# Modulation as row sums of a feature-major table, the first norm by feature blocks, five units fed as the chunks come

## The reference

```python
mod = c @ ada_w[l] + ada_b[l]                      # 1024 -> 6 * 1024
sh1, sc1, gt1, sh2, sc2, gt2 = [m[:, None, :] for m in jnp.split(mod, 6, axis=-1)]
h = rmsnorm(x, norm1_g[l]) * (1.0 + sc1) + sh1
p = h @ w_in[l]
xr, yr, q, k, v, ga, gb = jnp.split(p, cuts, axis=-1)
q = head_rmsnorm(q.reshape(b_, s_, ATT_HEADS, HEAD_DIM), q_norm_g[l])
k = head_rmsnorm(k.reshape(b_, s_, ATT_HEADS, HEAD_DIM), k_norm_g[l])
y_b = stick_breaking_attention(q, k, v)            # strictly causal, suffix sums of log(1 - beta)
mix = jax.nn.sigmoid(ga) * y_a + jax.nn.sigmoid(gb) * y_b
x = x + gt1 * (mix @ w_out[l])
h2 = rmsnorm(x, norm2_g[l]) * (1.0 + sc2) + sh2    # the second norm, then the feed-forward part
```

## Time and profile before

| | us |
|---|---|
| runs | 1677.64, 1678.43, 1678.77; median 1678.43 |
| the profiled execution | 1679.01, of which span 1677.2 |
| granted TensorE clock, mean over the span | 0.988 of full speed |
| busy: PE, DVE, ACT, POOL | 1631.8, 1001.8, 805.3, 811.4 |
| read from HBM | 163.45 MB, 99 GB/s over the span |
| first product of a unit | 42.63 |

### The profile page before, as it was taken

One profiled execution on the slowest core, in us unless ns is written; L12 is line 12 of the kernel. 1 busy time (PEld: TensorE's weight loads), 2 busy tenths in 40 slices (PEclk: granted clock), 3 DMA queues, 4 the chain that ended last, 5 costly groups with the idle time before them and its releaser, 6 DMA issues.

```text
span 1677.2 us, 19574 instructions
## 1 busy us (share of the span) xinstructions
PE 1631.8 (97%) x7252; PEld 1331.1 (79%) x7252; DVE 1001.8 (60%) x1172; ACT 805.3 (48%) x1010; POOL 811.4 (48%) x583
## 2 busy tenths in 40 slices
PE   3999999999999999999999999999999999999997
PEld 2778787777778888888888888888888888888885
DVE  6687898878657728616634767566337554255541
ACT  2565666666544324424352333677554444244442
POOL 2254454454645545455565454554584352453525
PEclk7999999999999999999999999999999999999999
DMA  9333332443323233233233231211132221321312
GB/s 372 126 123 127 124 116 77 138 138 100 101 82 103 90 109 100 88 125 100 90 100 95 76 107 62 73 56 57 64 99 77 63 88 55 109 88 52 100 50 76
DMA packets 46462, 166.81 MB, mean 99 GB/s; under 512 B 5152, under 2 KB 5280, under 8 KB 45856
## 3 DMA queue, kind: packets, MB, share of 16 engines
q1 hardware_dynamic: 46368, 165.57, 29.8%
HBM read 163.45 MB, written 2.10 MB: 99 GB/s over the span
## 4 chain that ended last, share of the span: by engine, by line
PE 91%; DVE 5%; ACT 1%; DMA 1%; issue 1%; POOL 1%; SPq 0%; POOLq 0%; ACTq 0%; DVEq 0%
PE lin L658 17%; PE lin L660 16%; PE lin L659 16%; PE big L659 7%; PE big L658 7%; PE big L660 7%; DVE scr L1611 1%; PE big L771 1%; PE m_o L789 1%; PE big L1076 1%; PE big L1078 1%; PE big L1077 1%; DMA scr<-ada 1%; DVE scr L1719 1%; PE m_a L964 1%
## 5 line engine op out<-in xcount | busy, mean ns | idle before, releaser
L624 POOL TENSOR_TENSOR w_lo<-raw,w_hi 128x512 fp32r<-128x512 f32 x200 | 291.5, 1458 | 622.0 <-ACT w_hi L1115 621.7
L658 PE MATMUL lin<-h_hi,w_hi 128*128 128x512 f32 x936 | 370.4, 396 | 2.1 <-POOL w_lo L627 1.9
L660 PE MATMUL lin<-h_hi,w_lo 128*128 128x512 f32 x936 | 365.4, 390 | 0.0
L659 PE MATMUL lin<-h_lo,w_hi 128*128 128x512 f32 x936 | 365.2, 390 | 0.0
L627 POOL TENSOR_TENSOR w_lo<-raw,w_hi 128x512 fp32r<-128x512 f32 x209 | 309.9, 1483 | 13.9 <-ACT w_hi L1115 13.9
L1115 ACT ACTIVATE w_hi<-raw 128x1024 fp32r<-128x1024 f32 (+1 forms) x209 | 217.6, 1041 | 203.0 <-DMA raw<-weights 52.1
L658 PEld LDWEIGHTS lin<-h_hi,w_hi 128*128 128x128 f32 x936 | 176.2, 188 | 41.1 <-issue 2.7
L659 PEld LDWEIGHTS lin<-h_lo,w_hi 128*128 128x128 f32 x936 | 176.1, 188 | 38.1 <-issue 2.2
L660 PEld LDWEIGHTS lin<-h_hi,w_lo 128*128 128x128 f32 x936 | 176.0, 188 | 37.2
L624 POOL TENSOR_TENSOR qk_hl<-raw,qk_hl 128x512 fp32r<-128x512 f32 x43 | 59.9, 1392 | 126.8 <-ACT qk_hl L1115 126.8
L658 PE MATMUL lin<-y_hi,w_hi 128*128 128x512 f32 x260 | 101.5, 391 | 0.0
(11 more groups left out here) (507 smaller groups left out, 3401.1 us busy)
## 6 DMA issues: line engine op xcount, KB each, us to landing
raw<-weights SPq DMA_DIRECT2D x245, 512.0 KB, 3.5
slab<-ada SPq DMA_DIRECT2D x32, 512.0 KB, 4.4
scr<-ada SPq DMA_DIRECT2D x16, 512.0 KB, 6.3
raw<-weights SPq DMA_DIRECT2D x10, 256.0 KB, 2.7
x<-x_t SPq DMA_DIRECT2D x2, 1024.0 KB, 6.4
out_t<-scr SPq DMA_DIRECT2D x8, 256.0 KB, 2.6
raw<-weights SPq DMA_DIRECT2D x4, 448.0 KB, 3.4
rgw<-rg_w SPq DMA_DIRECT2D x1, 1024.0 KB, 8.6
```

The source lines that it names most:

```text
L624: nc.gpsimd.tensor_tensor(lo[:, 0:4 * P], raw[:, s, 0:4 * P], hi[:, 0:4 * P].bitcast(F32), ALU.subtract).then_inc(w_half, 1)
L658: nc.tensor.matmul(psum_of(n), wh, hi(k), start=(k == 0), stop=False)
L659: nc.tensor.matmul(psum_of(n), wh, lo(k), start=False, stop=False)
L660: last = nc.tensor.matmul(psum_of(n), wl, hi(k), start=False, stop=(k == nk - 1))
```

## The change

Five things change together.

1. *The table is turned.* The host lays `ada_w` out feature-major: a chunk now holds 128 output features on the partitions and all 1024 values of c's index on the columns. One DVE instruction, `tensor_tensor_reduce`, multiplies it by c, written out along every row, and adds up the row, with the bias as the start (`modulate`). The accumulators, PE's one-column products and the additions of the bias go. c's row is made at the start: DVE spreads c over the diagonal (`c_spread`), two products with ones turn it (`c_turned`), ACT copies it to SBUF (`c_copied`). The first 16 sums read it from PSUM, the later 32 from SBUF.
2. *The first norm by blocks.* The chunks come as scale 0, shift 0, scale 1, shift 1 and so on. DVE makes two sums and then the h block, eight times. The root is written to PSUM, and the blocks read it there.
3. *Five units at once.* PE takes q0, k0, v0, q1 and k1 chunk by chunk as the blocks come, by a table (`LANES`). v0, q1 and k1 get the three banks of `big`, and two more homes for weights lie in y_hi and y_lo. The first five packs are loaded between the modulation chunks.
4. *Order in head 1.* v1 comes before the scores of head 0, which wait for the copies of q1 and k1 as well; ACT copies k1 before it takes up the scores. Chunks 16 to 18 stand behind v1 in the ring, 19 to 21 between xr0 and yr0.
5. *Fillers.* Three products after the squares and twelve behind the second norm's sum (`keep_clock`), whose results nobody reads. Small: the constants are loaded in two parts, x signals in two halves, DVE's small preparations stand before the sums.

The diff, cut to its core:

```diff
@@ ring_plan @@
-            units += [("q", 0, 8), ("k", 0, 8), ("v", 0, 8), ("ada", a, 8), ("ada", a + 1, 8), ("q", 1, 8),
-                      ("ada", a + 2, 8), ("k", 1, 8), ("ada", a + 3, 8), ("v", 1, 8), ("ada", a + 4, 8)]
+            units += [("q", 0, 8), ("k", 0, 8), ("v", 0, 8), ("q", 1, 8), ("k", 1, 8), ("v", 1, 8)]
+            units += [("ada", a + i, 8) for i in range(3)] + [("xr", 0, 8)] + [("ada", a + i, 8) for i in (3, 4)]
             continue
...
+TABLE = [b for k in range(DK) for b in (DK + k, k)] + list(range(ADA_FIRST, NADA))
+SIDE = {("v", 0): 2, ("q", 1): 3, ("k", 1): 4}
+
+LANES = ((("q", 0), (1, 2, 3, 4, 5, 6, 7, 8)), (("k", 0), (0, 2, 3, 4, 5, 6, 7, 8)),
+         (("v", 0), (0, 0, 3, 4, 5, 6, 7, 8)), (("q", 1), (0, 0, 0, 0, 3, 6, 7, 8)),
+         (("k", 1), (0, 0, 0, 0, 0, 0, 3, 8)))
@@ SP @@
             for i in range(ADA_FIRST):
+                if i in (0, 2, 4, 9, 12):
+                    load_weights((0, 2, 4, 9, 12).index(i))
@@ PE @@
+            def keep_clock(n, bank, ones, moving):
+
+                for _ in range(n):
+                    nc.tensor.matmul(bank, ones, moving, start=True, stop=True)
...
-            modulation(0)
-            modulation(1)
+            keep_clock(3, lin[:, 0], c_("ones"), x[:, 0])
+            for step in range(DK):
+                pe.wait_ge(h_low, step + 1)
+                for (kind, j), due in LANES:
+                    for k in range(due[step - 1] if step else 0, due[step]):
+                        chunk(kind, j, k)
...
-                if h == 0:
-                    pair(("q", 0), ("k", 0), H, L, normed(0))
-                elif h < HEADS:
+                if h > 1:
                     unit("q", h, H, L)
-                if h == 1:
-                    unit("k", h, H, L)
+                if g == 0:
+                    unit("v", h, H, L)
                 if g >= 0:
                     pe.wait_ge(kq_normed, 2 * g + 2)
                     if g > 0:
                         pe.wait_ge(gates_read, g)
+                    else:
+                        pe.wait_ge(q_copied, 2)
+                        pe.wait_ge(k_copied, 2)
                     scores(g)
...
-                    if h % 2 == 0:
-                        modulation(1 + h // 2)
...
             norm_sum(0)
-            modulation(5)
+            keep_clock(12, m_o[:], ones_r[:], y_hi[:, 0])
@@ ACT @@
+                if k == 3:
+                    act.wait_ge(c_turned, 1)
+                    nc.scalar.activation(c_row, c_row_ps, ACT.Copy).then_inc(c_copied, 1)
+                    act.wait_ge(c_copied, 1)
+            norm_root(square_used, 8, D, m_a[:])
+            for k in range(DK):
+                if k in (0, 1, 2):
+                    split_ahead(0, k)
+                if k in (4, 5):
+                    split_ahead(0, k - 1)
+                high(0, k)
...
+                if h < 2:
+                    keys(h)
                 if g >= 0:
                     act.wait_ge(z_done, g + 1)
@@ DVE @@
-            def accumulate(a):
+            def modulate(i):
...
+                v.tensor_tensor_reduce(out=src, in0=src, in1=row, scale=scale, scalar=first, op0=M, op1=AD,
+                                       accum_out=to).then_inc(ada_used, 1)
+                dve.wait_ge(ada_used, counted(ada_used))
...
+            dve.wait_ge(c_copied, 1)
+            for k in range(DK + 1):
+                if k < DK:
+                    modulate(2 * k)
+                    modulate(2 * k + 1)
+                    if k == 0:
+                        dve.wait_ge(norm_rooted, 1)
+                    v.scalar_tensor_tensor(out=tmp[:, k % 4], in0=x[:, k], scalar=sm(A1 + k), in1=m_a[:],
+                                           op0=M, op1=M).then_inc(pre_h, 1)
+                    dve.wait_ge(pre_h, counted(pre_h))
+                if k > 0:
+                    e = k - 1
+                    dve.wait_ge(h_high, e + 1)
+                    v.scalar_tensor_tensor(out=h_lo[:, e], in0=tmp[:, e % 4], scalar=sm(MOD + e),
+                                           in1=h_hi[:, e].bitcast(F32), op0=AD, op1=SU).then_inc(h_low, 1)
+                    dve.wait_ge(h_low, counted(h_low))
...
                 else:
-                    accumulate(ADA_FIRST)
-                    accumulate(ADA_FIRST + 1)
+                    modulate(ADA_FIRST)
...
-                accumulate(ADA_FIRST + 4 * h + 2)
+                modulate(ADA_FIRST + 4 * h + 1)
+                modulate(ADA_FIRST + 4 * h + 2)
```

More of the change, by code:

```diff
@@ L180, in bank_plan @@
         if kind in ("rv", "vn"):
+            continue
+        if (kind, j) in SIDE:
+            bank[n], before[n] = SIDE[kind, j], None
+            last[bank[n]] = n
             continue
@@ L211, in build @@
         par_loaded = sem("par_loaded")
-        x_loaded = sem("x_loaded")
+        x_loaded = [sem(f"x_loaded{i}") for i in range(2)]
         cst_loaded = sem("cst_loaded")
+        diff_loaded = sem("diff_loaded")
         rgw_loaded = sem("rgw_loaded")
@@ L716, in norm_sum @@
                     .then_inc(norm_summed, 1)
-            def modulation(g):
-                pe.wait_ge(acc_ready, g + 1)
-                acc = acc_first if g == 1 else acc_even
-                for m in range(DK):
-                    out = m_o[:, 8 * g + m:8 * g + m + 1] if g < 2 else m_b[:, 8 * g - 16 + m:8 * g - 15 + m]
-                    last = nc.tensor.matmul(out, acc[:, m // 4, (m % 4) * P:(m % 4 + 1) * P], c_("ones")[:, 0:1],
-                                            start=True, stop=True)
-                last.then_inc(mod_done, 1)
             def pair(a, b, hi, lo, ready):
@@ L757, in normed, with chunk @@
                 return ready
+            def chunk(kind, j, k):
+                n = UNIT[(kind, j)]
+                if k == 0:
+                    pe.wait_ge(w_split, PACK[n] + 1)
+                w_h, w_l = weights_of(n)
+                wh, wl = w_h[:, k * P:(k + 1) * P], w_l[:, k * P:(k + 1) * P]
+                nc.tensor.matmul(psum_of(n), wh, H(k), start=(k == 0), stop=False)
+                nc.tensor.matmul(psum_of(n), wh, L(k), start=False, stop=False)
+                last = nc.tensor.matmul(psum_of(n), wl, H(k), start=False, stop=(k == DK - 1))
+                if k == DK - 1:
+                    last.then_inc(unit_done, 1)
             pe.wait_ge(cst_loaded, 16)
-            pe.wait_ge(par_loaded, 16)
+            pe.wait_ge(c_spread, 1)
+            for i in range(2):
+                last = nc.tensor.matmul(m_bo[:, i], c_("ones"), c_row[:, i * T:(i + 1) * T], start=True, stop=True)
+            last.then_inc(c_turned, 1)
             for k in range(DK):
                 square(k + 1, k == 0, k == DK - 1)
-            modulation(0)
-            modulation(1)
+            keep_clock(3, lin[:, 0], c_("ones"), x[:, 0])
[4 more added lines that the diff above has]
+                        chunk(kind, j, k)
             def scores(g):
@@ L1190, in gate, with high @@
                 act.wait_ge(rgate_done, counted(rgate_done))
-            def highs(r):
-                for k in range(DK):
-                    act.wait_ge(pre_h, DK * r + k + 1)
-                    nc.scalar.activation(h_hi[:, k], tmp[:, k % 4], ACT.Identity,
-                                         bias=sm(MOD + 24 * r + k)).then_inc(h_high, 1)
-                    act.wait_ge(h_high, counted(h_high))
+            def high(r, k):
+                act.wait_ge(pre_h, DK * r + k + 1)
+                nc.scalar.activation(h_hi[:, k], tmp[:, k % 4], ACT.Identity,
+                                     bias=sm(MOD + 24 * r + k)).then_inc(h_high, 1)
+                act.wait_ge(h_high, counted(h_high))
             act.wait_ge(consts_set, 2)
@@ L1328, in _ @@
             norm_root(norm_summed, 1, D)
-            highs(1)
+            for k in range(DK):
+                high(1, k)
             for t in range(THIRDS):
```

140 lines of the change are left out of this document (65 added, 75 removed).

## The result

The changed kernel takes 1685.17 us (median of 5 runs, 1681.40 to 1686.51) against 1678.43 before: 6.7 us more, ratio 1.0036, 95% interval 1.0025 to 1.0047. 1678.0 was forecast. The profiled execution is the slowest of the five: 1686.51, span 1684.5, 7.3 more than the span before.

The account below looks back on a forecast made before the run. TensorE, busy 97% of 1677.2 us, was taken as the bound. Front +5.0, modulation products -5.1 and fillers -0.3 gave -0.4 us, so 1678.0; the forecast's own range was 1674.5 to 1681.5, the wider one 1666 to 1684.

Parts of the forecast that it names:

- the front: Everything up to head 0's turned weights: 2.8 us behind, plus 2.2 for the low clock, summed to +5.0 us.
- Part 1: Modulation and first norm on DVE: steps of 4.5 us, five units complete at 61.7 instead of 74.47, a 12.8 us lead.
- Part 2: Behind the five units: head 0's scores wait for q1 and k1, start 4.7 us late; turned weights 2.8 us behind.
- the pack named: yr 0's weight pack, loaded behind chunks 19 to 21, holds ACT before q1's copy some 8 us; 4.70 from issue to start.
- The 2.2 us for the clock: Behind the wait at head 0's turned weights, PE stays at the low clock level, costing 2.2 us more.
- Part 3: After the front: three groups of modulation products gone from the full PE stage, -5.1 us; fillers -0.3; the rest nothing.
- Twelve fillers: Products of 0.23 us in the wait for the second norm, keeping 2.4 GHz at best: 0.3 us won.
- (1): Rival at head 0's scores: yr's pack is there in time, the lead stays, scores start at 69.0; 1665 us, chance 0.15.
- (2): Rival on the front's sums: they are short, 1.23 us, with 17 on the path, 4.1 us less; 1674 us, chance 0.17.
- (3): Rival: accumulating sums halve in speed; 1681 us if only three behind q0, 1696 if all 17; chance 0.13.
- (4): Rival: PE at 1.2 GHz into the fifth step, or both waits cost 6 us of low level; 1682, shared chance 0.10.

Follow-up runs that it names:

- experiments 1 and 2: Ring of two PSUM banks started at bank 1 instead of 0: in the changed kernel, 1681.50 us; in the kernel before, 1681.55 us.
- Kernel 9: Changed kernel with ring started at bank 1, yr0's pack ahead of chunks 19 to 21, first half of x in two transfers, head 1 reordered: 1667.86 us.
- kernel 4: Changed kernel with both repairs: ring of two banks started at bank 1, yr0's weight pack loaded ahead of chunks 19 to 21; 1671.35 us.
- experiment 8: Against kernel 4: ACT splits yr0's pack behind q1's and k1's copies, DVE builds the low part of k1's squares ahead of the shares; 1668.73 us.
- experiments 5 and 6: Two runs against kernel 4: first half of x in two smaller transfers, 1669.98 us; both groups of filler products taken out, 1672.06 us.
- experiment 7: Against kernel 4: the sixteen modulation sums of the front read c's row from SBUF instead of PSUM; 1676.31 us.
- kernel 3: Changed kernel with yr0's weight pack loaded right behind xr0's, ahead of modulation chunks 19 to 21; 1672.30 us.

## Why the prediction was wrong

**The step that failed** is the claim that the whole sum can be made at the turned weights of head 0 because "what is left to do there is the same in both kernels", with "Between 98 and 474 us it never waits" carried over to the changed kernel. The profile of before supports the second for before. But `SIDE` in the diff takes three units out of a turn of two, and the order of PE shows nothing of it. The term stood at nothing and cost 3.5 us in the profiled execution, shown from both sides (experiments 1 and 2); 1.9 of it is the wait and the rest the clock behind it. With it the forecast would have been 1681.5.

That is half of the miss. The other half, 3.6 us, is the front: its mechanism held, and its terms were too small, as parts 1 and 2 show. Neither half alone leads out of the range that was stated.

**Part 1, the step: right, its start wrong.** Low parts 4.28 us apart, forecast 4.5. A sum with its reading 1.32 to 1.39 us, forecast 1.47, inside the bounds 1.23 and 2.4. The root came at 21.45, forecast 17.4. Kernel 9 helps to divide these 4.0 us: there ACT starts on x at 7.7, PE starts the squares at 8.88, and the root is out at 18.67. So 1.3 us stand even with x early. The forecast let the squares run from 7.8, but until 8.9 to 9.1 PE turns c's row (5.37, for 3.75), two products that it had at nothing. The late x costs 1.0 (PE's squares at 9.91 for 8.88), and the low clock 1.7 (5.69 us for eight records, there 3.96). From root to q0 ready it was 38.2, forecast 38.9; q0 was ready at 59.7 and all five units at 65.0, forecast 56.3 and 61.7.

**Part 2: the mechanism right, its size too small.** ACT waited 9.99 us for the pack named, forecast some 8; PE idled 12.2 us, forecast 10; the scores were 10.3 us later than before, forecast 4.7; the turned weights 8.6 later, forecast 2.8, and 2.2 more for the clock behind them. Two terms account for it. The start, 3.4 us late at q0 (59.67 for 56.3). And the pack, 6.70 us from SP's load (74.28) to ACT's start, where the 4.70 of the row before was taken: 2.0. From ACT's start to the scores (3.8, forecast 3.7) and from the scores to the turned weights (21.6, forecast 21.4) the working held. The 2.2 us for the clock were charged behind the turned weights. In the trace the low clock lies ahead of them, behind a wait of 3.57 us for k1's squares that the forecast did not have, and together they filled the 4 us that PE was to wait in front of the turned weights: yr0 and the exponential end together at 106.4. So that the front missed by 3.6 only is luck in part: the turned weights were 5.8 later than worked out, less the 2.2 charged for a low clock that did not come.

**Part 3: right.** 4.8 us won between the turned weights of head 0 and of head 7, forecast 5.1. Twelve fillers: 0.1 in this execution, forecast 0.3. Between the turned weights of head 0 and of head 7 no wait of PE shows behind the second part of the constants or the longer sums in the heads; what the missing 0.3 of the 5.1 is stays open.

**Rivals.** (1), the pack is there in time, is false for the change, and as a repair it is what the chip gives: 1671.35 with both repairs, 1665 as worked out. In the profiled execution of kernel 4 (1668.86, the fastest of its five) the turned weights start at 92.1 and not at 88.2, which is all of the difference to 1665: the scores start at 71.0 for 69.0, since ACT still splits ahead of the copies (experiment 8), they take 4.0 us at the low clock, and PE waits 3.6 us for k1's squares behind them. The start is not to blame: q0 was ready at 55.8, forecast 56.3. The other 2.5 us are the distance of that execution from the median, probably the varying start and clock of experiments 5 and 6. (2), short sums, half true: the sums are 0.1 us shorter than forecast, 17 of them 1.9 us. (3), the halving: false. 1.284 us is the short form with accumulation and two SBUF operands, against 1.284 for the old sum without. The halving of the Trainium skill's "Points that are easy to get wrong" (Vector Engine (DVE) Microarchitecture Reference) does not show here; that rule names `S2S2D2_STT`, and the trace records the sum as CUSTOM_DVE_ANT_0, so whether it holds for an accumulating `scalar_tensor_tensor` was not tested. The stretching to 2.2 us is another matter, seen with and without accumulation. (4), half clock in the last steps, true in a small way: 44 to 48 us, 1.2 us, in some executions.

**The account.** The profiled execution came out 7.9 us above the 1678.6 worked out for it. The bank is 3.5 of them, the front 3.6 (8.6 for 5.0), part 3's products 0.3, the fillers 0.2: 7.6, and 0.3 is left open.

## What to carry to other kernels

Where buffers or banks are given in turn, taking an odd number of users out of the turn changes the partner of every later user; print the plan (who had this bank before) for both kernels and look at the places where two turns meet. A wait of 1.7 us can cost twice that if the clock falls behind it. A load queue in order is part of the path of everything behind it: before a load is put behind others that wait for sums, ask which engine waits for it with what queued behind. And a lead won at the front is worth only as much as the next load or split that is tied to the old pace; both repairs here are a line or two, and they turn 6.7 us lost into 7.3 us won.

## What the runs showed of the hardware

- A row sum (`tensor_tensor_reduce`) of 128x1024 float32 takes 1.28 us, or 1.34 where its scale is read from a table, and the reading of the accumulator 0.08 us; its row starts 0.07 before the main row ends.
- With one operand in PSUM it kept 1.28 to 1.34 in all 16 cases, eight of them beside GpSimd's splits; with two in SBUF six of 16 went to 2.2 us, and GpSimd's own instructions from 1.27 to 2.2 (experiment 7).
- A wait of PE for a bank whose reader is done late appears as "issue", without a releaser (1.73 and 1.74 us). Behind it the granted clock was 0.53 for 3.5 us in the changed kernel and 1.00 in kernel 3: the same wait, two outcomes.
- ACT could start on the first half of x between 7.9 and 10.0 us in seven profiled executions of kernels with the same loads, and PE left its low level between the first and the ninth square record. The changed kernel's five runs spread by 5.1 us, the six kernels with its loads of x by 2.7 to 4.8, those with x in smaller transfers by 1.6 and 0.8; the kernel before by 1.1 in its first five runs and by 2.1 to 2.9 in the larger sets. That the start is the cause of the spread is likely but not shown: five runs are few. The windows' clock column says 1.00 for this stretch in either case: at the very start the durations of the products are the better sign.
